# Two gated blocks with the weights standing and the tokens moving, in a small hybrid model's forward pass on one core

## What is computed

```python
def rmsnorm(x, gain):
    xf = x.astype(jnp.float32)
    y = xf * lax.rsqrt(jnp.mean(xf * xf, axis=-1, keepdims=True) + EPS)
    return (y * gain.astype(jnp.float32)).astype(x.dtype)

def swiglu(h, w_gate, w_up, w_down):
    return (jax.nn.silu(h @ w_gate) * (h @ w_up)) @ w_down

# in second_block, for each of the two layers:
h = rmsnorm(x, ffn_pre_gain[i])
x = x + rmsnorm(swiglu(h, ffn_w_gate[i], ffn_w_up[i], ffn_w_down[i]), ffn_post_gain[i])
```

## Time and profile before

| what | us |
|---|---|
| median of 3 timed runs | 1165.41 |
| lowest and highest of them | 1156.53, 1168.57 |
| the profiled execution's own time | 1152.62 |
| its span in the trace | 1150.8 |
| TensorE busy (matmuls) | 1102.9 |
| VectorE busy | 783.4 |
| ScalarE busy | 598.0 |

### The profile page before, as it was taken

The page is one execution under the profiler, slowest core; times in us unless marked ns, Lnnn a source line. Parts: engine busy times, 40 slices in busy tenths (PEclk is TensorE's granted clock), DMA queues, the critical chain, the costliest instruction groups (busy, mean ns, idle before and its releaser), DMA issues.

```text
span 1150.8 us, 18422 instructions
## 1 busy us (share of the span) xinstructions
PE 1102.9 (96%) x7620; PEld 910.4 (79%) x7620; DVE 783.4 (68%) x1268; ACT 598.0 (52%) x927; POOL 119.6 (10%) x122
## 2 busy tenths in 40 slices
PE   7999999999999999999998999999999799999997
PEld 6777878777888888887877887878878688888786
DVE  6747874767677775658566896887578867555553
ACT  6566533243665663565655654445672267345441
POOL 0405050500000000000000000012105400000000
PEclk9999999999999999999999999999999999999999
DMA  8533322024654555555323654555531245555551
GB/s 316 183 115 121 129 75 75 21 74 146 200 184 165 183 178 189 183 166 192 122 90 110 255 185 151 182 198 190 175 130 58 76 165 183 189 180 190 192 200 57
DMA packets 49668, 177.50 MB, mean 154 GB/s; under 512 B 5648, under 2 KB 6288, under 8 KB 49328
## 3 DMA queue, kind: packets, MB, share of 16 engines
q1 hardware_dynamic: 49440, 175.79, 45.0%
q10 hardware_dynamic: 144, 0.52, 0.1%
HBM read 175.25 MB, written 1.05 MB: 153 GB/s over the span
## 4 chain that ended last, share of the span: by engine, by line
PE 79%; DVE 12%; ACT 6%; issue 2%; POOL 1%; DMA 0%; SPq 0%; DVEq 0%; ACTq 0%
PE wps L2679 22%; PE wps L2681 21%; PE wps L2680 21%; PE tps L2668 4%; DVE wlo L1817 3%; ACT whi L1420 1%; PE wps L3123 1%; PE tps L2909 1%; DVE arena L2039 1%; PE tps L2914 1%; PE tps L2725 1%; DVE bt L2434 1%; PE tps L3089 1%; DVE bt L2445 1%; PE tps L2886 1%
## 5 line engine op out<-in xcount | busy, mean ns | idle before, releaser
L1817 DVE TENSOR_TENSOR wlo<-raw,whi 128x1024 fp32r<-128x1024 f32 (+1 forms) x322 | 390.4, 1232 | 174.1 <-ACT whi L1420 172.7
L2679 PE MATMUL wps<-whi,a_hi 128*128 128x512 f32 (+1 forms) x1008 | 400.5, 397 | 4.6 <-DVE a_lo L1825 2.3
L2681 PE MATMUL wps<-wlo,a_hi 128*128 128x512 f32 (+1 forms) x1008 | 391.9, 389 | 0.0
L2680 PE MATMUL wps<-whi,a_lo 128*128 128x512 f32 (+1 forms) x1008 | 391.1, 388 | 0.0
L1420 ACT ACTIVATE whi<-raw 128x1024 fp32r<-128x1024 f32 (+1 forms) x322 | 327.2, 1053 | 76.2 <-PE wps L2681 76.1
L2679 PEld LDWEIGHTS wps<-whi,a_hi 128*128 128x128 f32 x1008 | 189.3, 188 | 45.7 <-issue 5.9
L2681 PEld LDWEIGHTS wps<-wlo,a_hi 128*128 128x128 f32 x1008 | 189.2, 188 | 40.1
L2680 PEld LDWEIGHTS wps<-whi,a_lo 128*128 128x128 f32 x1008 | 189.6, 188 | 36.8 <-issue 0.5
L2679 PE MATMUL wps<-whi,f_hi 128*128 128x512 f32 x264 | 103.3, 391 | 0.0
L2681 PE MATMUL wps<-wlo,f_hi 128*128 128x512 f32 x264 | 102.8, 389 | 0.0
L2680 PE MATMUL wps<-whi,f_lo 128*128 128x512 f32 x264 | 102.7, 389 | 0.0
(11 more groups left out here) (419 smaller groups left out, 1247.4 us busy)
## 6 DMA issues: line engine op xcount, KB each, us to landing
raw<-in_w_dn SPq DMA_DIRECT2D x22, 512.0 KB, 3.2
raw<-in_w_0dn SPq DMA_DIRECT2D x22, 512.0 KB, 3.2
raw<-in_w_1dn SPq DMA_DIRECT2D x22, 512.0 KB, 3.2
raw<-in_w_ua SPq DMA_DIRECT2D x20, 512.0 KB, 3.2
raw<-in_w_ub SPq DMA_DIRECT2D x20, 512.0 KB, 3.3
raw<-in_w_0ug SPq DMA_DIRECT2D x20, 512.0 KB, 3.3
raw<-in_w_0uu SPq DMA_DIRECT2D x20, 512.0 KB, 3.3
raw<-in_w_1ug SPq DMA_DIRECT2D x20, 512.0 KB, 3.2
```

The source lines that it names most:

```text
L1817: V.tensor_tensor(t.wlo[n % NR][:, 0:w], t.raw[n % NR][:, 0:w], t.whi[n % NH][:, 0:w].bitcast(F32), ALU.subtract).then_inc(m.done(s.dve_lo ...
L2679: T.matmul(o, xh, wh, start=first, stop=False)
L2680: T.matmul(o, xl, wh, start=False, stop=False)
L2681: mm = T.matmul(o, xh, wl, start=False, stop=last)
```

## The change

From the second group on, both gated blocks swap the operands. In `stand` 128 columns of weights stand in the array and 256 tokens move. The sums come out with 128 channels on partitions and the 256 tokens along the free side, two such tiles to a bank. So they already lie as the down product wants them, and no transposes are needed. A slab is now 2 tiles of rows x 4 blocks of 128 columns x 3 = 24 matmuls of 256 columns. The factor 1/rms can no longer be a scale per partition: it must be a row. `root_row` makes it once per block from the column in `t.st` with two matmuls against the identity, and ScalarE copies it to `sqj`. The gating is then, for each of the two banks u of a group, with gt[u] = 128 x 512 in the second half of h:

- gate_scale (VectorE): gt = gate sums x row; gate_silu (ScalarE): Silu of gt, in place; gate_row (VectorE): gt = gt x row
- gate_times (VectorE): gt = gt x up sums; gate_hi (ScalarE): f_hi = copy of gt; gate_lo (VectorE): f_lo = gt - f_hi

They are steps of generators in `background`: gate_scale and gate_silu after slab 1 (u = 0) and slab 2 (u = 1) of the up stream, gate_row after slabs 3 and 4, gate_times and gate_hi after slabs 1 and 2 of the next gate stream, gate_lo one slab later each. For the tail stream all of it goes beside the first four slabs of `dn0`. The first group stays as it was, because its activations come ready one token half at a time.

```diff
+STANDING = (0, 1)
...
             for sub in range(2):
-                for j in range(2):
-                    use(n, kp, j, sub, sub == 1 and j == 1)
+                if standing:
+                    for c in range(4):
+                        stand(n, kp, c, sub)
+                else:
+                    for j in range(2):
+                        use(n, kp, j, sub, sub == 1 and j == 1)
...
+    def make_row():
+        while norm["tok"] is None:
+            yield
+        b, r = bank(), norm["tok"]
+        emit("root_row", r, b.name, b.free)
+        b.free = (("row", r),)
...
+    def gate_begin(l, i, n, r, name, banks):
+        for u in range(n):
+            emit("gate_scale", l, i, u, r, name, banks[u].name)
+            banks[u].free = (("gate_scale", l, i, u),)
+            emit("gate_silu", l, i, u)
+            yield
+        for u in range(n):
+            emit("gate_row", l, i, u, r)
+            yield
+
+    def gate_end(l, ffn, i, n, name, banks):
+        for u in range(n):
+            b, k = banks[u], 4 * i + 2 * u
+            emit("gate_times", l, i, u, name, u if n == 2 else 1, b.name)
+            b.free = (("gate_times", l, i, u),)
+            emit("gate_hi", l, i, u, ffn.name)
+            yield
+            emit("gate_lo", l, i, u, ffn.name)
+            ffn.tok[k] = ffn.tok[k + 1] = ("gate_lo", l, i, u)
+
+    def standing_groups(l, ffn):
+        def at_end(banks):
+            yield from gate_begin(l, 5, 1, r, f"{l}ut", banks[0:1])
+            yield from gate_end(l, ffn, 5, 1, f"{l}ut", banks[1:2])
...
+        for i in range(1, 5):
+            banks = whole(stream(f"{l}ug{i}", 8, main, standing=True))
+            finish_of(gates)
+            gates.append(gate_begin(l, i, 2, r, f"{l}ug{i}", banks))
+            background.append(gates[0])
+            banks = whole(stream(f"{l}uu{i}", 8, main, standing=True))
+            finish_of(gates)
+            gates.append(gate_end(l, ffn, i, 2, f"{l}uu{i}", banks))
+            background.append(gates[0])
+        banks = whole(stream(f"{l}ut", 8, main, standing=True))
+        finish_of(gates)
+        background.append(at_end(banks))
...
-        for i in range(5):
+        for i in range(1 if l in STANDING else 5):
...
+            if l in STANDING:
+                background.append(make_row())
             banks = whole(stream(up, 8, main))
...
+        if l in STANDING:
+            standing_groups(l, ffn)
+            return postnorm([f"{l}dn0", f"{l}dn1"], 22, ffn, then, **more)
...
+    def root_row(r, b, freed):
+        act.wait_ge(*m.at("root_row", r))
+        activate(t.row[r][:, :], t.bank[b][:, 0:S], ACT.Copy).then_inc(m.done(s.act_out, "row", r), 1)
...
+    def gate_scale(l, i, u, r, name, b):
+        dve.wait_ge(*m.at("row", r))
+        dve.wait_ge(*m.at("grp", name, u))
+        V.tensor_tensor(t.gt[u], by2(t.bank[b][:, :]), t.row[r][:, :].unsqueeze(1).to_broadcast([P, 2, S]), ALU.mult).then_inc(
+            m.done(s.dve_out, "gate_scale", l, i, u), 1)
...
+    def gate_times(l, i, u, name, half, b):
+        dve.wait_ge(*m.at("gate_row", l, i, u))
+        dve.wait_ge(*m.at("grp", name, half))
+        V.tensor_tensor(t.gt[u], t.gt[u], by2(t.bank[b][:, :]), ALU.mult).then_inc(m.done(s.dve_out, "gate_times", l, i, u), 1)
...
+    def stand(name, n, k, c, b, acts, k0, first, last, done, ready, freed):
+        w, sub = SLABS[n][2], k % 2
+        cols = slice(sub * w + c * P, sub * w + (c + 1) * P)
+        wh, wl = t.whi[n % NH][:, cols], t.wlo[n % NR][:, cols]
+        xh, xl = (a[:, k0 + k, :] for a in t.acts[acts])
+        o = t.bank[b][:, (c % 2) * S:(c % 2 + 1) * S]
...
+        T.matmul(o, wh, xh, start=first and c % 2 == 0, stop=False)
+        T.matmul(o, wh, xl, start=False, stop=False)
+        mm = T.matmul(o, wl, xh, start=False, stop=last and c % 2 == 1)
...
+    def root_row(r, b, freed):
+        wait_all(freed)
+        pe.wait_ge(*m.at("root", r))
+        for j in range(2):
+            mm = T.matmul(t.bank[b][:, j * P:(j + 1) * P], t.st[:, 2 + j:3 + j].to_broadcast([P, P]), t.con[:, 0:P], start=j == 0, stop=j == 1)
+        mm.then_inc(m.done(s.pe_side, "root_row", r), 1)
```

More of the change, by code:

```diff
@@ L204, in both_sides, with stream @@
         return tok if isinstance(tok, list) else [tok, tok]
-    def stream(name, nk, acts, after=None, banks=None):
+    def stream(name, nk, acts, after=None, banks=None, standing=False):
         if banks is None:
@@ L222, in beside, with stand @@
                     background.remove(g)
+        def stand(n, kp, c, sub):
+            assert SLABS[n][0:2] == (name, kp), (SLABS[n], name, kp)
+            k = 2 * kp + sub
+            first, last = k == 0, k == nk - 1
+            emit("stand", name, n, k, c, banks[c // 2].name, acts.name, acts.k0, first, last, sub == 1 and c == 3,
+                 both_sides(acts.tok[k]), banks[c // 2].free if first else ())
         nkp = nk // 2
@@ L776, in postnorm, with finish_of @@
         return done, second
+    def gate_begin(l, i, n, r, name, banks):
[20 more added lines that the diff above has]
+            yield from gate_end(l, ffn, 5, 1, f"{l}ut", banks[1:2])
+        assert norm["tok"] is not None
+        r = norm["tok"]
+        gates = []
+        for i in range(1, 5):
[10 more added lines that the diff above has]
+        background.append(at_end(banks))
+    def finish_of(gates):
+        for g in gates:
+            if g in background:
+                background.remove(g)
+                whole(g)
+        gates.clear()
     def swiglu(l, second, then=None, **more):
@@ L1264, in place @@
         hidden("f2", s5)
+    t.gt = [by2(t.h[:, u, 512:1024]) for u in range(2)]
     t.sg = [t.h[:, :, 512 * i:512 * (i + 1)] for i in range(2)]
+    rows = t.sqj[:, 0:S]
+    t.row = {2: rows, 4: rows, 6: rows}
     t.src = {"x": t.x, "h": t.h, "yb": t.yb, "fq": t.fq, "fk": t.fk, "sg0": t.sg[0], "sg1": t.sg[1], "mq": t.mq, "mk": t.mk}
@@ L1630, in conv_hi, with gate_silu, gate_hi @@
         activate(t.acts["f0"][0][:, k:k + 2, :], t.cv[u][:, :, :], ACT.Copy).then_inc(m.done(s.act_out, "conv_hi", i, u), 1)
+    @part
+    def gate_silu(l, i, u):
+        act.wait_ge(*m.at("gate_scale", l, i, u))
+        activate(t.gt[u], t.gt[u], ACT.Silu).then_inc(m.done(s.act_out, "gate_silu", l, i, u), 1)
+    @part
+    def gate_hi(l, i, u, acts):
+        k = 4 * i + 2 * u
+        act.wait_ge(*m.at("gate_times", l, i, u))
+        activate(t.acts[acts][0][:, k:k + 2, :], t.gt[u], ACT.Copy).then_inc(m.done(s.act_out, "gate_hi", l, i, u), 1)
     last_square = []
@@ L2687, in product @@
             mm.then_inc(m.done(s.pe_sums, "slab", n), 1)
+    @part
+    def stand(name, n, k, c, b, acts, k0, first, last, done, ready, freed):
[4 more added lines that the diff above has]
+        o = t.bank[b][:, (c % 2) * S:(c % 2 + 1) * S]
+        pe.wait_ge(*m.at("lo", n))
+        wait_all(ready)
+        wait_all(freed)
+        T.matmul(o, wh, xh, start=first and c % 2 == 0, stop=False)
+        T.matmul(o, wh, xl, start=False, stop=False)
+        mm = T.matmul(o, wl, xh, start=False, stop=last and c % 2 == 1)
+        if last and c % 2:
+            mm.then_inc(m.done(s.pe_sums, "grp", name, c // 2), 1)
+            if done:
+                m.also(("slab", n), ("grp", name, c // 2))
+        elif done:
+            mm.then_inc(m.done(s.pe_sums, "slab", n), 1)
+    @part
+    def root_row(r, b, freed):
+        wait_all(freed)
+        pe.wait_ge(*m.at("root", r))
+        for j in range(2):
+            mm = T.matmul(t.bank[b][:, j * P:(j + 1) * P], t.st[:, 2 + j:3 + j].to_broadcast([P, P]), t.con[:, 0:P], start=j == 0, stop=j == 1)
+        mm.then_inc(m.done(s.pe_side, "root_row", r), 1)
     def turn_pair(p, src, kb, b, freed, ready):
```

15 lines of the change are left out of this document (added).

## The result

The change made the kernel slower: median 1179.51 us (four runs, 1174.18 to 1185.63) against 1162.72 (four runs, 1156.53 to 1168.57), ratio 1.0181 with the interval 1.0135 to 1.0227. (A ratio here is estimated from the timed runs; it is not the quotient of the two medians, which is 1.0144.) The forecast was 1166.9 us and no change. The profiled execution took 1182.22 us.

What follows compares the result with a forecast made beforehand. TensorE, busy 96% of the span, was taken as the bound, VectorE second. Terms +11.4 - 7.1 - 3.4 + 0.6 = +1.5 us, put on the median 1165.4, gave 1166.9 us, no measurable change; range 1152 to 1180.

Steps and rivals of the forecast that it cites:

- Parts 1 to 3: Gated blocks on TensorE: 256-column matmuls +11.4 us, transposes gone from group two on -7.1, tail stream's end without gap -3.4.
- rival (a): Block products: the second matmul over the same weights loses its fixed cost; sum -6.2 us, 1160.7 us; chance 0.08.
- rival (c): Block products: a weight load isn't hidden behind 256 columns; sum +122 us, about 1288; chance 0.02.
- The rule that the prediction weighs: Matmul spacing from the Trainium skill; by it the 72 slabs would add 2.2 us instead of 11.4.
- this sign of being right: Between tail stream and down product: no idle time of TensorE.
- part 5: VectorE's eight gate operations a group at 0.60 us: 23.0 us against TensorE's 23.0 in block 0, cost 0; ScalarE 0.
- Part 2: Groups two to five lose their transposes: eight bunches of 0.89 us, -7.1 us.
- Part 4: Factor as a row, two 128-column matmuls per block: 0.3 us a block, +0.6 us, bounds 0 and 1.2, no wait.
- the sign of 100% from 706 to 754 us: Block 0: VectorE near 100% busy there, with TensorE still without a wait for wlo.
- The working of the cover: Block 0: three slabs already split ahead of TensorE, 8.6 us, absorb VectorE's backlog before TensorE stalls.
- Rival (b): Block 0: VectorE falls behind at 1.53 us a gate operation, stalling TensorE 12.5 us; sum +14.0, 1179.4 us; chance 0.07.

Runs made afterwards that it cites:

- e3: The change with gate_silu and gate_hi put one slab later, behind the next split (gate_row and gate_lo moved along): 1161.31 us, ratio 1.0019 to the kernel before.
- e1: The change in block 1 only, block 0 left as in the kernel before: 1158.03 us, ratio 1.0009 to the kernel before.
- e8: The change with only gate_silu put one slab later, gate_hi still directly behind gate_times: 1170.23 us, ratio 1.012 to the kernel before.
- e4: The change with 12 S5 table products in block 0 on an eighth of their elements (output differs): 1168.27 us, ratio 1.0081 to the kernel before.
- e7: The change with each split one slab further ahead, LOOK 4 in place of 3: 1182.21 us, ratio 1.0242 to the kernel before.

## Why the prediction was wrong, point by point

**Parts 1 to 3 were right on TensorE's side.** TensorE in the changed kernel, block 0, the first and the last of 16 products of 256 columns beside the earlier trace rows:

```profile
701.12 0.28 PE L2818 MATMUL wps<-a_lo,whi 128*128 128x256 f32 x1
...
702.91 0.28 PE L2818 MATMUL wps<-a_lo,whi 128*128 128x256 f32 x1
```

15 distances, 0.119 us each; 0.1200 was used. The second of two products over the same weights isn't cheaper (L2817 to L2818 is 0.12 us as well), so rival (a) is out. The loads hide, at 0.19 us each while the products start every 0.12, so rival (c) is out. The rule that the prediction weighs, columns by 2.4 GHz plus 2.5 ns, is given in the section that it names (the Trainium skill, TensorE: Matmul & The Clock Gate, section Back-to-back issue gap) for an isolated matmul. For a stream of loads and matmuls the section gives 131 ns at 512 columns. The 226.8 ns of the earlier trace rows fit neither. The end of the tail stream in block 1:

```profile
1113.43 0.28 PE L2819 MATMUL wps<-a_hi,wlo 128*128 128x256 f32 x1
1113.55 0.40 PE L2797 MATMUL wps<-whi,f_hi 128*128 128x512 f32 x1
```

No transposes and no wait; the down product starts 0.12 us behind the last block product. In block 0 the transposes are gone too, but there the change to the down product is just where the longest wait for wlo falls, 2.25 us (790.79 to 793.32, shown in the last section): this sign of being right failed in block 0, by the fault of part 5. Part 2 wasn't measured by itself; that the sum of the parts comes out (below) speaks for it.

**Part 4 was mis-sized: 2.6 us instead of 0.6.** The bounds given for it ended at 1.2. The row in block 0 and in block 1:

```profile
659.63 0.39 PE L2799 MATMUL wps<-wlo,a_hi 128*128 128x512 f32 x1
661.42 0.71 PE L2832 MATMUL tps<-con,st 128*128 128x128 f32 x4 [1.40 <-DVE st L1901]
...
662.20 0.40 PE L2798 MATMUL wps<-whi,a_lo 128*128 128x512 f32 x1
```

```profile
1000.14 0.39 PE L2799 MATMUL wps<-wlo,a_hi 128*128 128x512 f32 x1
...
1001.05 0.39 PE L2798 MATMUL wps<-whi,a_lo 128*128 128x512 f32 x1
```

The two matmuls stand as one row of four records in block 0. In block 1 they cost 0.46 us: 1000.14 to 1001.05 less the two distances of 0.2268. In block 0 it is 662.20 − 659.63 − 0.45 = 2.12 us, 1.40 of which are a wait for the root. The prediction had rows for the root in block 1 alone and took "no wait" for both. With this the blocks' own terms are 5.7 − 3.6 − 1.7 + 2.1 = +2.5 us (block 0) and 5.7 − 3.6 − 1.7 + 0.5 = +0.9 (block 1). Measured: +2.0 for block 0 without handoffs (e3) and +0.8 for block 1. The sum on TensorE's side was sound.

**Part 5 is the step that failed**, in two of its sentences. "ScalarE keeps its count ... at half load ..., so 0": load is not the point, order is. And "The waits that are added are each issued a slab behind their releaser" is true for gate_row and gate_lo, and false for gate_silu and gate_hi: these stand in ScalarE's queue directly behind the release, and ahead of the next whi. I had named what is queued behind the waiting instruction for VectorE but not for ScalarE. There VectorE's next split is queued, so VectorE waits for ScalarE, which waited for VectorE, four times a group. 0.63 + 1.04 us, of which 0.09 overlap (Silu starts at 743.64, whi at 744.18), and some 0.04 us of signalling at either end, make the 1.65 us; that is 6.6 us a group. VectorE's cycle becomes 23.0 + 6.6 = 29.6 us; gate_scale comes at 712.24, 742.92 and 772.84, 30.7 and 29.9 us apart (the longer one holds the wait of 2.41 us). Rows of before showed such a handoff, the 1.82 us that VectorE waited for f_hi; there it came once a group, and I read the durations of the rows and not their brackets. With VectorE waiting, the sign of 100% from 706 to 754 us failed as well: it is busy 22.65 of 30 us from 712 to 742.

The working of the cover then holds: 7.7 + 6.9 = 14.6 us too late by 772.8, less 8.6, is 6.0 us of stall; the stretches up to 772 show 0.4 + 5.4. Of block 0's 19.2 us, the profile then gives 2.5 for the block's own terms, 10.7 of TensorE's idle time from 712 to 800, and 3.4 by the clock (0.12 of 28 us). The 2.6 left are what a wait costs besides its idle time. The idle time begins only when the last matmul has ended, 0.28 us after its start, when the next would have started after 0.12; and the first product behind a wait takes 0.22 us to the next (776.46 to 776.68) in place of 0.12. That is 0.26 us a wait, 2.9 us for the 11 waits, an estimate from these rows.

**Rival (b) had the place and even the time (1179.4 us), but not the mechanism.** It asked for a gate operation of 1.53 us, decided "from about 1.0 us an operation", and got 0.07 because that price is unlikely; it is 0.60. The right question would have been what a gate operation costs VectorE with its wait: (0.60 × 8 + 6.6) / 8 = 1.43 us, above the limit.

That the measured median, 1179.5 us, lies within the range up to 1180 is luck: the range reached there only to take in rival (b), whose price was wrong. The forecast itself was +1.5 us, and the two medians of the result lie 16.8 us apart.

In block 1 the same handoffs cost nothing measurable (216.5 us with them, and 216.5 in e3 without), where VectorE has no tables and is busy 24.2 of 40 us.

**What stays open.** How much of the whole kernel's loss the clock adds. Over the span, the time at the lower level (worked out from the granted clock of stretches of 1 us) is 10 us in the profile of before and 37 in that of the change, but 15 in e1, 19 in e3 and 41 in e8, mostly in code that is the same in all. In block 0 of the change it is 6.8 us, the 3.4 us of loss above. No run kept the stalls and held the clock.

## What to carry to other kernels

When two engines hand a tile back and forth, write the two queues side by side and ask of every waiting instruction what stands behind it, on the engine that is idle too: an engine at half load delays everything behind a wait at its head. Put the consumer of a fresh result behind the next independent piece of work, not at once behind its producer. Price an added instruction on a busy engine with the waits around it, and check a "no wait" in each place where the code runs, not in one.

## What the runs showed of the hardware that I had not expected

**The clock fell after some short waits and not after others.** TensorE in block 0 of the changed kernel, two pairs of waits in the block products:

```profile
746.53 0.39 PE L2817 MATMUL wps<-a_hi,whi 128*128 128x256 f32 x1 [0.86 <-DVE wlo L1908]
...
748.27 0.39 PE L2817 MATMUL wps<-a_hi,whi 128*128 128x256 f32 x1 [0.76 <-DVE h L2310]
...
776.46 0.39 PE L2817 MATMUL wps<-a_hi,whi 128*128 128x256 f32 x1 [0.86 <-DVE wlo L1908]
...
778.19 0.38 PE L2817 MATMUL wps<-a_hi,whi 128*128 128x256 f32 x1 [0.76 <-DVE h L2310]
```

The pairs are alike to 0.01 us. After the first the granted clock stays at 1.00, though TensorE stands still six times for 5.4 us in all from 742 to 772. After the second it falls from about 778.7 to 782 us, 3.4 us at the lower level:

```profile
778.00:782.00 4.00, 3.81 (x19) 3.81 (x20) 2.36 (x3) 3.48 (x4) 0.00 (x0) 0.58 0.10 40
```

And at the change to the down product:

```profile
790.79 0.28 PE L2819 MATMUL wps<-a_hi,wlo 128*128 128x256 f32 x1
793.32 0.50 PE L2797 MATMUL wps<-whi,f_hi 128*128 128x512 f32 x1 [2.25 <-DVE wlo L1908]
...
795.32 0.50 PE L2797 MATMUL wps<-whi,f_hi 128*128 128x512 f32 x1 [1.03 <-DVE h L2323]
...
796.01 0.63 PE L2799 MATMUL wps<-wlo,f_hi 128*128 128x512 f32 x1
796.44 0.63 PE L2797 MATMUL wps<-whi,f_hi 128*128 128x512 f32 x1
...
799.54 0.39 PE L2799 MATMUL wps<-wlo,f_hi 128*128 128x512 f32 x1
```

It waits 2.25 and, after three matmuls, 1.03 us. From 796.01 on the same products come 0.43 us apart instead of 0.23: the lower level of the clock, 1.2 GHz, and 0.23 again from 799.54. Two short waits, 3.3 us in all, are followed by 3.5 us at half speed, which cost 1.75 us more: half as much again. In before, 0.48 and 0.35 us had no such effect. So no single wait here had to be long for the clock to fall, but the waits alone don't say when it does.

**VectorE beside GpSimd.** The split of 1024 elements takes 1.22 us alone. In the change GpSimd starts a step at 782.22 and one at 785.14 us, and the splits that start just behind, at 782.66 and 785.59, take 2.07 and 2.31 us (the same two lengths in e4). In before the order is the other way round:

```profile
761.77 1.22 DVE L1817 TENSOR_TENSOR wlo<-raw,whi 128x1024 fp32r<-128x1024 f32 x1
761.87 2.03 POOL L2619 TENSOR_TENSOR rot<-pr,con 128x512 f32<-128x512 f32 x1
```

Here the split starts first and keeps its 1.22 us, and GpSimd's step takes 2.03 us, where the same step takes 1.04 at 779.17 us. In these rows the one that starts second is the one that takes longer.

**A deeper look-ahead isn't free:** LOOK = 4 moved the waits from wlo to the banks and saved nothing (e7).
